# Attention values of two heads at a time, projected with the tokens on the partitions

## The reference

```python
h = rms_norm(x, g_mix[l])
z = h @ w_in[l]
qa, ka, va, ga, ub, vb, qc, kc, vc, gates = split_cols(z)
...
qc = rms_normalize(qc.reshape(B, S, N_DIL, DIL_HEADS, DIL_HD)) * dil_q_norm_g[l]
kc = rms_normalize(kc.reshape(B, S, N_DIL, DIL_HEADS, DIL_HD)) * dil_k_norm_g[l]
vc = vc.reshape(B, S, N_DIL, DIL_HEADS, DIL_HD)
for gi, (win, dil) in enumerate(((128, 1), (512, 4), (2048, 16))):
    o, lse = dilated_window_attention(qc[:, :, gi], kc[:, :, gi], vc[:, :, gi], win, dil)
wts = softmax(stack(lses), axis=0)
yc = sum(wts[..., None] * stack(outs), axis=0)
```

## Time and profile before

| | |
|---|---|
| time, median of 3 runs | 1910.86 us (1910.6 to 1911.08) |
| the profiled execution's own time | 1910.71 us |
| its span | 1908.9 us |
| busy PE / DVE / ACT / POOL | 99% / 65% / 44% / 5% of the span |
| granted PE clock | 1.00 in all 40 slices |
| DMA, mean | 155 GB/s |

### The profile page before, as it was taken

One profiled execution on the slowest core, in us unless ns is written; L12 is line 12 of the kernel. 1 busy time (PEld: TensorE's weight loads), 2 busy tenths in 40 slices (PEclk: granted clock), 3 DMA queues, 4 the chain that ended last, 5 costly groups with the idle time before them and its releaser, 6 DMA issues. The chain is left out here.

```text
span 1908.9 us, 26594 instructions
## 1 busy us (share of the span) xinstructions
PE 1894.6 (99%) x10632; PEld 1699.3 (89%) x10632; DVE 1246.4 (65%) x1625; ACT 844.4 (44%) x1186; POOL 96.9 (5%) x148
## 2 busy tenths in 40 slices
PE   8999999999999999999999999999999999999999
PEld 7888888888888899899888888888888888998998
DVE  7767767746566786377576667677365657863775
ACT  5544444524234464155335444345242344642554
POOL 0000001111111000000000000011111110000000
PEclk9999999999999999999999999999999999999999
DMA  5322356787777355366333222577777773653663
GB/s 203 95 78 67 89 135 182 190 221 206 205 204 207 93 177 173 100 191 198 120 100 95 67 78 83 144 199 185 210 211 211 194 201 92 193 159 107 201 210 122
DMA packets 85897, 295.68 MB, mean 155 GB/s; under 512 B 20368, under 2 KB 20624, under 8 KB 84624
## 3 DMA queue, kind: packets, MB, share of 16 engines
q1 hardware_dynamic: 73104, 218.49, 36.8%
q0 software_dynamic: 12672, 75.51, 17.1%
HBM read 291.79 MB, written 77.66 MB: 194 GB/s over the span
## 5 line engine op out<-in xcount | busy, mean ns | idle before, releaser
L1057 ACT ACTIVATE w_high<-raw 128x1024 fp32r<-128x1024 f32 x396 | 418.3, 1057 | 791.7 <-PE bank L847 663.1
L1266 DVE TENSOR_TENSOR w_low<-raw,w_high 128x1024 fp32r<-128x1024 f32 x396 | 483.0, 1222 | 147.6 <-ACT w_high L1057 141.0
L847 PE MATMUL bank<-h_high,w_high 128*128 128x512 f32 x1408 | 543.5, 386 | 8.9 <-DVE h_low L1271 8.2
L847 PE MATMUL bank<-h_low,w_high 128*128 128x512 f32 x1408 | 534.3, 379 | 0.0
L847 PE MATMUL bank<-h_high,w_low 128*128 128x512 f32 x1408 | 534.1, 379 | 0.0
L847 PEld LDWEIGHTS bank<-h_high,w_high 128*128 128x128 f32 x1408 | 266.7, 189 | 47.0 <-issue 8.1
L847 PEld LDWEIGHTS bank<-h_high,w_low 128*128 128x128 f32 x1408 | 266.6, 189 | 38.0
L847 PEld LDWEIGHTS bank<-h_low,w_high 128*128 128x128 f32 x1408 | 266.8, 189 | 36.2
L847 PE MATMUL bank<-in_high,w_high 128*128 128x512 f32 x672 | 255.0, 379 | 0.0
L847 PE MATMUL bank<-in_low,w_high 128*128 128x512 f32 x672 | 254.7, 379 | 0.0
L847 PE MATMUL bank<-in_high,w_low 128*128 128x512 f32 x672 | 254.7, 379 | 0.0
(11 more groups left out here) (163 smaller groups left out, 2344.3 us busy)
## 6 DMA issues: line engine op xcount, KB each, us to landing
raw<-weights SPq DMA_DIRECT2D x325, 512.0 KB, 4.1
weight_sums<-weights POOLq DMA_DIRECT2D x108, 512.0 KB, 6.1
raw<-weight_sums SPq DMA_DIRECT2D x72, 512.0 KB, 3.8
weight_sums<-weight_sums POOLq DMA_DIRECT2D x36, 512.0 KB, 4.1
turned<-rows SPq DMA_DIRECT2D x3, 768.0 KB, 6.8
xT<-x_t SPq DMA_DIRECT2D x8, 256.0 KB, 5.4
decay_sb<-decay SPq DMA_DIRECT2D x8, 256.0 KB, 5.0
out_t<-xT SPq DMA_DIRECT2D x8, 256.0 KB, 6.4
```

The source lines that it names most:

```text
L847: return pe.matmul(o, w, m, start=start, stop=stop)
L1057: act.activation(w_high[:, PART_SLOT[s], :, :], raw[:, s % RAW_SLOTS, :, :], ACT.Copy).then_inc(part_high_w.sem, 1)
L1266: dve.tensor_tensor(w_low[:, PART_SLOT[s], :, :], raw[:, s % RAW_SLOTS, :, :], w_high[:, PART_SLOT[s], :, :], ALU.subtract).then_inc(part_ ...
```

## The change

The v tiles of two heads h and h+1 are made together by `by_token`. In the even head four tiles "va" make groups 1 and 2 of both heads: the activations are stationary and read by phase (every fourth token), 512 columns of weights move, and the banks are a main bank, the two turn banks and the other main bank. In the odd head two tiles "vb" make group 0 of both heads with 256 columns, two token blocks to a turn bank. So heads have ten and eight tiles in turn; the tiles and slabs of a layer stay as many. ACT evacuates them with the norm's factor as a scale of the partition (`token_evac`), for which `("stat", "n", 0)` also sums by phase. `vtrans` of v is gone. The first k tile of an odd head goes to the statistics bank, `pv` of an even head comes five tiles later, and the last head's `weigh` and `ptrans` and retention's `rpv` move by a tile.

```diff
-        t += [("v", h, g) for g in range(N_GROUP)]
+        t += [("va", h // 2, j) for j in range(4)] if h % 2 == 0 else [("vb", h // 2, j) for j in range(2)]
...
+TOKEN_ROLES = {"va": 4, "vb": 2, "sv": 4}
+SCALED_ROLES = {"rq", "rk", "rv", "rg", "su", "gate", "fgate"}
...
-            if j > 0:
-                pre[t + 7 + j] += [("vtrans", "v", h, j)]
         pre[t + 6] += [("rstd", "cq", h)]
-        pre[t + 7] += [("scores", h, 0), ("scores", h, 1), ("expo", h, 0), ("vtrans", "v", h, 0)]
+        pre[t + 7] += [("scores", h, 0), ("scores", h, 1), ("expo", h, 0)]
...
-        pre[t + 13] += [("ptrans", h, 2), ("pv", h, 0), ("ptrans", h, 3)]
-        pre[t + 14] += [("pv", h, 1), ("pv", h, 2), ("high", "yc", h), ("low", "yc", h)]
+        pre[t + 11] += [("weigh", h)]
+        pre[t + 12] += [("ptrans", h, 0), ("ptrans", h, 1)]
+        pre[t + 13] += [("ptrans", h, 2), ("ptrans", h, 3)]
+        at = t + (13 if h % 2 else 18)
+        pre[at] += [("pv", h, 0)]
+        pre[at + 1] += [("pv", h, 1), ("pv", h, 2), ("high", "yc", h), ("low", "yc", h)]
...
+        def token_bank(base, role, p, b):
+
+            if role == "sv":
+                return (score_bank + [out_bank, stat_bank])[b][:, :]
+            if role == "vb":
+                return turn_bank[b // 2][:, b % 2 * 2 * P:(b % 2 + 1) * 2 * P]
+            first = AT["va", p, 0]
+            return [bank_of(base, first), turn_bank[0], turn_bank[1], bank_of(base, first - 1)][b][:, :]
...
+            if TILES[i][0] == "k" and TILES[i][1] % 2 == 1 and TILES[i][2] == 0:
+                return stat_bank
...
-            def by_token(base, i, j):
+            def by_token(base, i):
...
+                if role != "sv" and j == 0:
+                    n = sum(place[u] < place["main", i, 0, KT] for u in T_USERS)
+                    for u in T_USERS[n - 2:n]:
+                        wait_turned(pe, base, u)
+                if role == "va" and j == 0:
+                    wait_evacuated(pe, base, i - 2)
...
                     for b in range(BLK):
-                        hi, lo = (h[:, k, b * P:(b + 1) * P] for h in (h_high, h_low))
-                        o = token_bank[b][:, :]
-                        matmul(o, hi, wh, k == 0, False)
+                        if role == "va" and k == 0 and b == BLK - 1:
+                            wait_evacuated(pe, base, i - 1)
+                        hi, lo = (h[:, k, :].rearrange("p (i r) -> p r i", r=PHASES)[:, b, :] if role == "va" else
+                                  h[:, k, b * P:(b + 1) * P] for h in (h_high, h_low))
...
+                if key == ("n", 0):
+                    for r in range(PHASES):
+                        last = matmul(stat_bank[:, BLK + r:BLK + r + 1],
+                                      squares.rearrange("p (i r) -> p r i", r=PHASES)[:, r, :], ones[:, 0:1], True, True)
...
                         for b in range(BLK):
-                            act.activation(sg_v[:, b, :], token_bank[b][:, :], ACT.Gelu_apprx_tanh,
-                                           scale=rs[:, b:b + 1]).then_inc(values_ready.sem, 1)
+                            dst, col = {"va": (va[b], BLK + b), "vb": (vb[:, b, :], b), "sv": (sg_v[:, b, :], b)}[role]
+                            act.activation(dst, token_bank(base, role, p, b),
+                                           ACT.Gelu_apprx_tanh if role == "sv" else ACT.Copy,
+                                           scale=rs[:, col:col + 1]).then_inc(values_ready.sem, 1)
```

More of the change, by code:

```diff
@@ L221, in schedule @@
         post[t] += [("rotate", "rq", h)]
-        if h == 0:
-            pre[t + 2] += [("weigh", HEADS - 1)]
         post[t + 1] += [("rotate", "rk", h)]
[L226 to L231, removed]
-        pre[t + 4] += [("rscore", h, m) for m in range(2, BLK)]
[L233 to L236, removed]
+        pre[t + 3] += [("vtrans", "rv", h)] + [("rscore", h, m) for m in range(2)]
+        pre[t + 4] += [("rscore", h, m) for m in range(2, BLK)]
+        last = t + (7 if h == 0 else 6)
+        pre[last] += [("rpv", h), ("ocopy", h), ("square", "r", h), ("split_sq", "r", h)]
+        pre[last + 1] += [("rowstat", "r", h), ("rowstd", "r", h)]
+        post[last + 1] += [("rowinv", "r", h)]
+        post[last + 2] += [("rowscale", "r", h), ("high", "yr", h), ("low", "yr", h)]
     t = AT["sv", 0]
@@ L307, in schedule @@
             steps.append(("main", i, 0, len(BLOCKS[i])))
-        steps += splits + pre[i] + ([("evac", i)] if TILES[i][0] != "sv" else [("token_evac",)] if i == AT["sv", HEADS - 1] else [])
+        steps += splits + pre[i] + ([("evac", i)] if TILES[i][0] not in TOKEN_ROLES else
+                                [("token_evac", i)] if TILES[i][-1] == TOKEN_ROLES[TILES[i][0]] - 1 else [])
         steps += later + post[i]
@@ L448, in build @@
         qk = [work[:, j, :] for j in range(6)]
-        v_tok = [work[:, 6 + g, :].rearrange("p (b e) -> p b e", b=BLK) for g in range(N_GROUP)]
+        va = [values_rows[r // 2][:, r % 2, :] for r in range(PHASES)]
+        vb = work[:, 6:8, :].rearrange("p a (b e) -> p (a b) e", b=2)
         probs = work[:, 9:13, :].rearrange("p a (n k) -> p (a n) k", k=P)
@@ L598, in std_place, with wait_turned @@
             return prod[:, key[2], :] if key[2] < 2 else k_std2
+        place = {s: n for n, s in enumerate(STEPS)}
         def wait_turn_bank(pe, base, n):
-            if n < 2:
-                return
-            u = T_USERS[n - 2]
+            for i, in keys("token_evac"):
+                behind = [m for m, u in enumerate(T_USERS) if place[u] > place["token_evac", i]][:2]
+                if TILES[i][0] != "sv" and n in behind:
+                    pe.wait_ge(values_ready.sem, values_ready.at(base, *TILES[i][:-1], BLK - 1))
+            if n >= 2:
+                wait_turned(pe, base, T_USERS[n - 2])
+        def wait_turned(pe, base, u):
             if u[0] == "vtrans":
@@ L875, in by_token @@
                 slab = BLOCKS[i][0][0]
                 pe.wait_ge(part_low_w.sem, part_low_w.at(base, slab))
-                for kk in range(2):
-                    k = 2 * j + kk
-                    wh, wl = (in_turn(w[:, PART_SLOT[slab], 4 * kk:4 * kk + 4, :].rearrange("p c n -> p (c n)"))
+                inner = KT // TOKEN_ROLES[role]
+                wide = 8 // inner
+                for kk in range(inner):
+                    k = inner * j + kk
+                    wh, wl = (in_turn(w[:, PART_SLOT[slab], wide * kk:wide * (kk + 1), :].rearrange("p c n -> p (c n)"))
@@ L885, in by_token, with wait_bank @@
+                        o = token_bank(base, role, p, b)
+                        first, end = (b % 2 == 0, b % 2 == 1) if role == "vb" else (True, True)
+                        matmul(o, hi, wh, k == 0 and first, False)
                         matmul(o, hi, wl, False, False)
-                        last = matmul(o, lo, wh, False, k == KT - 1)
+                        last = matmul(o, lo, wh, False, k == KT - 1 and end)
                 last.then_inc(tile_done.sem, 1)
+            def wait_bank(base, i):
+                t = TILES[i]
+                if t[0] == "k" and t[1] % 2 == 1 and t[2] == 0:
+                    pe.wait_ge(std_ready.sem, std_ready.at(base, "cq", t[1] - 1))
+                elif t[0] == "k" and t[1] % 2 == 1:
+                    pe.wait_ge(values_ready.sem, values_ready.at(base, "va", t[1] // 2, {1: BLK - 1, 2: 0}[t[2]]))
+                else:
+                    same = [u for u in range(i) if TILES[u][0] not in TOKEN_ROLES and bank_of(base, u) is bank_of(base, i)]
+                    if same:
+                        wait_evacuated(pe, base, same[-1])
@@ L1647, in _weights @@
                 src, col, row0 = w_down[layer], t[2] * P, t[1] * FF_BLOCKS[0] * P
[L1648 removed]
+            elif t[0] in TOKEN_ROLES:
+                names = {"sv": [("sv", c) for c in range(HEADS)],
+                         "va": [("v", 2 * t[1] + h, g) for g in (1, 2) for h in range(2)],
+                         "vb": [("v", 2 * t[1] + h, 0) for h in range(2)]}[t[0]]
                 for s, place, i in blocks:
[L1650 to L1653 removed]
+                    wide = len(names)
+                    k = 8 // wide * t[-1] + i // wide
+                    values = np.concatenate([w_in[layer][k * P:(k + 1) * P, of(n):of(n) + P] for n in names], axis=1)
+                    values = values.reshape(P, wide * P // 2, 2).transpose(0, 2, 1).reshape(P, wide * P)
+                    out[layer * HOST_ROWS + SOURCE[s], :, place, :] = values[:, i % wide * P:(i % wide + 1) * P]
                 continue
```

57 lines of the change are left out of this document (25 added, 32 removed).

## The result

| | before | changed kernel |
|---|---|---|
| time, median | 1910.79 us (1910.6 to 1911.08, 4 runs) | **1938.18 us** (1936.62 to 1940.55, 4 runs) |
| ratio | | 1.0146, 95% interval 1.0133 to 1.016 |
| profiled execution, own time / span | 1910.71 / 1908.9 us | 1940.55 / 1938.7 us |

Slower, as forecast, but by 27 us and not by 10, and outside the range. The profiled execution is the slowest of the four; what follows is made against its span, +29.8 us.

The account below looks back on a forecast made before the run. PE bounds the kernel. Terms -9.8 + 1.5 + 1.6 + 11.7 + 3.8 + 1.2 = +10.0 us on 1910.7 gave 1920.7 us; own range 1916 to 1925, with rivals 1907 to 1927 at 0.8.

Parts of the forecast that it names:

- The bound, and distances instead of busy time: PE, busy 1894.6 of 1908.9 us, sets the span; its work is counted from start to start of instructions.
- Transposes, vb: On PE: removing the 24 groups of v transposes gives -9.8 us; vb's 384 matmuls of 256 columns add 1.5 us.
- work alone: PE's transposes, vb and sums by phase, without waits: -6.7 us; as a rival, 1904.0 us, chance 0.11.
- the second kind: Head 1 to 2, twice: PE waits because weigh comes later and ACT loads the exponential table first; +3.8 us.
- The three kinds of wait: New PE waits: even to odd head, four places, +11.7 us; head 1 to 2, +3.8; head 0 of each layer, +1.2.
- layer 1's late exchange: In layer 1 the exchange through DRAM lands later, so shift_exp waits longer; 0.9 us added once to the even-to-odd-head waits.
- the third kind: Head 0 of each layer: va's fourth token block waits for DVE to evacuate the third q tile; 2 x 0.6, +1.2 us.
- A load 2.1 times as long is 0.21 us and still fits beside a matmul of 0.216: nothing: In va, stationary loads of every fourth float, lengthened by DVE's strided ratio, stay hidden beside their matmuls; 0 us.
- The rival that had the loads right: Strided loads are not hidden: between +2 and +42 us on top, 1923 to 1963 us; chance 0.09.
- Costed at nothing: ACT's four evacuation copies of va, the weights' slabs and the late pv: no PE wait, 0 us.

Follow-up runs that it names:

- in_order_table_early: Changed kernel with va activations and norm squares read in token order, odd heads' first k sum a tile earlier, exponential table loaded early by a dummy: 1905.8 us, ratio 0.9976.
- va_in_order: Changed kernel with the va tiles' stationary activations read in token order instead of every fourth: 1929.88 us, ratio 1.0105.
- before_with_waits: Kernel before, with one PE wait added before the first transposes of probs of heads 0, 1 and 2, six in two layers: 1932.46 us, ratio 1.0116.
- before_phase_sums: Kernel before, with eight unread one-column products added behind the norm's sums, their stationary squares read with a stride of four: 1916.88 us, ratio 1.0033.

## Why the prediction was right in sign and wrong in size

- **The bound, and distances instead of busy time**: right. The 17 us by which PE got busier with less work are longer distances.
- **Transposes, vb**: right. `in_order_table_early` is the test of all that I called PE's work. It takes 1905.8 us, where work alone would give 1910.0 - 6.7 = 1903.3 beside its own before. The 2.5 between fit what its distances show of waits that are left: 2 x (1.13 - 0.68 + 1.23 - 0.81) = 1.7 of the second kind, and two waits of 0.4 of the third.
- **The three kinds of wait**: right in place, releaser and number; 10.5 + 4.2 + 0.7 = 15.4 us against 16.7. The 0.9 for layer 1's late exchange didn't come (3.31 and 3.29 there, 3.31 and 3.28 in layer 0), and the third kind was 0.36 a place and not 0.6. With the longer loads and the clock left out, the measured terms make +9.3 where the forecast has +10.0, so the sign was right for the reason given.
- **"A load 2.1 times as long is 0.21 us and still fits beside a matmul of 0.216: nothing"**: this step failed. The fit had a margin of 3%. The load is 0.233, and the pace of all 384 matmuls is then the load's. The ratio borrowed from DVE was not the fault: against the 0.111 of a product added in order, 0.233 is 2.1 times as long. The base was: 0.81/8 = 0.10 for one load, where the eight products added in order cost 0.111 each. With the sums, where nothing covers a load, the step costs 9.9 + 2.1 = 12.0 us by the table, or 8.6 + 2.1 = 10.7 by `va_in_order`. The rival that had the loads right held 1938 in its bounds, and I gave it 0.09. That it held 1938 is in part luck: with the loads alone the time would be some 1932.
- **The clock**: absent from the prediction altogether, and this is the second step that failed. I priced waits at their length. A wait of PE of 2.3 to 2.4 us, the shorter waits of head 1 to 2 in a row (0.80, 0.43 and 0.21), and the strided sums are followed by a stretch at 1.2 GHz in many places, 1.7 us each, 10.2 in the profiled execution. `before_with_waits` and `before_phase_sums`, which have nothing else of the change, show it for the waits and for the sums.
- **Costed at nothing** (four copies of va, late `pv`, slabs): right, no such wait appears.

With loads of 0.233 us the same sum, by the terms measured for vb, sums and waits, would have come to 1910.7 + 21.3 = 1932.0, and the clock makes the rest: 1942 with six stretches, against the 1940.55 of the profiled execution. Open is what decides whether the clock falls behind a given wait or group of sums: of equal ones some have it and some not. The four times of the changed kernel differ by 3.9 us in all. Their mean clocks say that the slowest has the most stretches; among the other three, all at 0.996, the count is not shown.

## What to carry to other kernels

When stationary operands get a stride, compare the load's own time at that stride with the matmul that covers it, and if the margin is a few per cent, measure one such load before believing in cover. Here every second float cost next to nothing and every fourth doubled the load. When a change makes PE wait, allow for a stretch at half clock behind each wait in the upper bound (here 1.7 us by the matmuls, behind waits of 2.3 us and behind shorter ones in a row), and look for it with short windows, since the page's slices are too long. Before two traces are compared to a microsecond, compare the start of the same step in both ahead of the first edit. And a change that only moves work should have each semaphore's queue walked as here: the forecast waits were where the walk put them, and a sum moved by one tile took them away.

## What the runs showed of the hardware that was not expected

- A weight load of 128 columns with a product of one column costs 0.111 us in order, 0.119 with a stride of two floats and 0.233 with four; its row in the trace shows it too (189, 196 and 335 ns).
- Strided loads under 512-column matmuls leave the granted clock at 1.00, but eight of them with one column each were followed by a stretch at 0.50 in 9 of 10 places of the five traces that have them.
- Behind a wait of 2.3 us between full tiles, with nothing else changed, the clock was at 0.50 at four of six places. The shorter waits of head 1 to 2 (0.80, 0.43 and 0.21 us in a row) had it behind them too, in both layers of the changed kernel.
- The first 7 to 14 matmuls of each trace stand 0.43 us apart, half the pace, while the view gives their granted clock as 1.00: the distances show what the column does not.
